# Projections of a hybrid diffusion layer: 26 weight slabs as seven half products of sums in place of eight

## The reference, cut to what matters

```
proj = h @ p["w_in"]                              # h is 384 x 1024
conv_out = _short_conv(proj[..., :D_CONV], ...)   # nine groups of channels, width 3
... hyena, HGRN2, SSD and gated DeltaNet on the parts of proj and conv_out ...
lifted = jnp.einsum("blnc,ncd->blnd", branches, p["w_branch"])
gates = jax.nn.sigmoid(merge).reshape(bsz, L, N_BRANCH, D_MODEL)
mixed = jnp.einsum("blnd,blnd->bld", gates, lifted)
return mixed @ p["w_out"], s_hg, s_ssd, s_gdn
```

## Time and profile before

| | us |
|---|---|
| median of 3 runs | 1486.23 |
| lowest, highest run | 1482.81, 1486.43 |
| span of the profiled execution | 1486.3 |
| PE busy | 1454.8 |
| DVE busy | 463.0 |
| ACT busy | 394.0 |
| POOL busy | 87.4 |

### The profile page before, as it was taken

The page is one execution under the profiler, slowest core; times in us unless marked ns, Lnnn a source line. Parts: engine busy times, 40 slices in busy tenths (PEclk is TensorE's granted clock), DMA queues, the critical chain, the costliest instruction groups (busy, mean ns, idle before and its releaser), DMA issues.

```text
span 1486.3 us, 19276 instructions
## 1 busy us (share of the span) xinstructions
PE 1454.8 (98%) x7422; PEld 914.7 (62%) x7422; DVE 463.0 (31%) x984; ACT 394.0 (27%) x897; POOL 87.4 (6%) x76
## 2 busy tenths in 40 slices
PE   6999999999999999999999999999999999999996
PEld 2565678776786666777865875444555555555553
DVE  3437232663244235323110373211111211221114
ACT  3222112222343233213320232222222222322223
POOL 0000010000021103222111000000000000000001
PEclk9999999999999999999999999999999999999998
DMA  9540423213112328510133335999999898999981
GB/s 372 160 128 8 137 68 113 86 57 113 57 57 86 125 88 308 216 57 29 57 99 118 121 145 210 369 413 382 377 377 382 358 378 355 379 379 380 379 341 43
DMA packets 103944, 308.82 MB, mean 208 GB/s; under 512 B 9168, under 2 KB 69328, under 8 KB 75344
## 3 DMA queue, kind: packets, MB, share of 16 engines
q1 hardware_dynamic: 97552, 304.89, 53.7%
q10 hardware_dynamic: 6336, 3.15, 0.7%
HBM read 304.87 MB, written 3.15 MB: 207 GB/s over the span
## 4 chain that ended last, share of the span: by engine, by line
PE 96%; DMA 2%; DVE 1%; ACT 0%; POOL 0%; issue 0%; SPq 0%; POOLq 0%; DVEq 0%
PE banks L554 43%; PE banks L2480 15%; PE banks L2517 8%; PE banks L2389 7%; PE banks L2381 6%; PE banks L913 4%; PE banks L561 2%; PE banks L1057 1%; PE banks L767 1%; DMA ring<-in_ada_w 1%; PE banks L594 1%; PE banks L662 1%; DMA ring<-in_w_in 1%; PE banks L1105 1%; PE banks L2400 1%; PE banks L657 1%
## 5 line engine op out<-in xcount | busy, mean ns | idle before, releaser
L554 PE MATMUL banks<-hT,ring 128*128 128x384 f32 x1200 | 393.7, 486 | 0.0
L554 PEld LDWEIGHTS banks<-hT,ring 128*128 128x128 f32 x1200 | 226.3, 190 | 153.5 <-issue 2.4
L2480 PE MATMUL banks<-w,xg 128*64 128x512 f32 (+1 forms) x1312 | 234.8, 596 | 0.0
L2480 PEld LDWEIGHTS banks<-w,xg 128*64 128x64 f32 (+1 forms) x1312 | 73.7, 127 | 154.9 <-issue 135.8
L2517 PE MATMUL banks<-w,hidT 128*64 128x512 f32 (+1 forms) x656 | 120.7, 597 | 0.3 <-ACT hidT L2557 0.3
L2389 PE MATMUL banks<-y,selT 128*128 128x512 f32 x384 | 104.4, 407 | 0.0
L2389 PEld LDWEIGHTS banks<-y,selT 128*128 128x128 f32 x384 | 67.3, 188 | 37.7 <-issue 26.2
L554 PE MATMUL banks<-yT,ring 128*128 128x384 f32 x256 | 87.4, 486 | 0.0
L2656 DVE TENSOR_TENSOR y<-banks,y 128x512 fp32r<-128x512 f32 x66 | 45.6, 691 | 133.3 <-ACT y L2573 133.3
L554 PE MATMUL banks<-ring,hT 128*128 128x256 f32 x384 | 86.2, 387 | 0.0
L554 PEld LDWEIGHTS banks<-ring,hT 128*128 128x128 f32 x384 | 74.4, 195 | 10.6
(11 more groups left out here) (404 smaller groups left out, 1478.1 us busy)
## 6 DMA issues: line engine op xcount, KB each, us to landing
w<-in_exp_w SPq DMA_DIRECT2D x198, 1024.0 KB, 8.6
ring<-in_w_in SPq DMA_DIRECT2D x46, 1024.0 KB, 5.4
ring<-in_ada_w SPq DMA_DIRECT2D x24, 1024.0 KB, 7.5
ring<-in_w_branch SPq DMA_DIRECT2D x8, 1024.0 KB, 6.5
ring<-in_w_out SPq DMA_DIRECT2D x4, 1024.0 KB, 6.4
arena<-in_sh_w SPq DMA_DIRECT2D x3, 1024.0 KB, 7.4
arena<-in_t_last_layer SPq DMA_DIRECT2D x1, 1024.0 KB, 8.2
x<-in_x_sample SPq DMA_DIRECT2D x2, 512.0 KB, 11.6
```

The lines of the kernel that those rows point to most:

```text
L554: last = mm(out, lhsT=lhsT, rhs=rhs, start=i == 0, stop=i == len(pairs) - 1)
L2480: ins = mm(ps[lo:hi, :], lhsT=xg[:, k, a_ * P + lo:a_ * P + hi], rhs=w13[:, a_, u, :, k, :], start=k == 0, stop=k == KD - 1)
```

## The change

Both the slab (8 k blocks x 2 channel blocks) and the tokens (8 k blocks x 384 tokens) are cut in two along both sides: weights into a11, a12, a21, a22 (first index channel block, second the half of k), tokens into b11, b12, b21, b22 (half of k, half of the tokens, 192 each). Eight products of halves become seven of sums, in Strassen's way. It is applied to 26 slabs: the two of each of `hy_x1`, `hy_x2`, `ssd_x`, `ssd_bc`, `gdn_k`, `gdn_q`, `gdn_v`, and the four of each of merge 1, 2 and 3. The rest (`hy_v`, merge 0, the `hg` groups, `ssd_z`, `gdn_g`) stays.

A pair is opened and closed on PE. It holds three banks from the first product to the last; each half product is 4 products of 192 columns:

```
+            def open_pair(*name):
+                i = pair_at[name]
+                slab(pe, name)
+                w = blocks(name)
+                pair_banks[name] = y, z, v = banks.hold(pe), banks.hold(pe), banks.hold(pe)
+                half_product(psum[:, v, 0:HALF], w[0][1], hT[:, 4:8, 0:HALF])
+                s_partial.on(half_product(psum[:, y, 0:HALF], w[0][0], hT[:, 0:4, 0:HALF]))
+                pe.wait_ge(s_tokens.sem, 4)
+                pe.wait_ge(s_combos.sem, 4 * i + 1)
+                s_partial.on(half_product(psum[:, z, 0:HALF], w[1][0], token_mix[:, 2]))
+                pe.wait_ge(s_combos.sem, 4 * i + 2)
+                pe.wait_ge(s_kept.sem, 4 * i + 1)
+                s_partial.on(half_product(psum[:, y, 0:HALF], combos[:, 1], token_mix[:, 1], False))
+            def close_pair(*name):
+                i = pair_at[name]
+                w = blocks(name)
+                y, z, v = pair_banks[name]
+                pe.wait_ge(s_kept.sem, 4 * i + 2)
+                half_product(psum[:, z, 0:HALF], w[1][1], token_mix[:, 3], False)
+                pe.wait_ge(s_combos.sem, 4 * i + 3)
+                pe.wait_ge(s_kept.sem, 4 * i + 3)
+                s_partial.on(half_product(psum[:, y, 0:HALF], combos[:, 0], token_mix[:, 0], False))
+                pe.wait_ge(s_combos.sem, 4 * i + 4)
+                pe.wait_ge(s_corner.sem, i + 1)
+                last = half_product(psum[:, v, 0:HALF], w[0][1], hT[:, 4:8, HALF:T])
+                banks.release_all(last, (v, y, z), name, "dve")
+                slab_done(name)
```

```
+            def keep(*name):
+                i = pair_at[name]
+                if i:
+                    banks.emptied(act, PAIRS[i - 1])
+                for n, (bank, to) in enumerate(((0, 0), (1, 1), (0, 2)), 1):
+                    act.wait_ge(s_partial.sem, 4 * i + n)
+                    s_kept.on(on(kept[:, to, :], psum[:, pair_banks[name][bank], 0:HALF], ACT.Copy))
+            def add_up(out, *name):
...
+                dve.wait_ge(s_kept.sem, 4 * i + 1)
+                s_corner.on(tt(out[:, 0, 0:HALF], kept[:, 0, :], v, ALU.add))
+                dve.wait_ge(s_kept.sem, 4 * i + 4)
+                lane.do(tt(out[:, 1, 0:HALF], kept[:, 2, :], z, ALU.add))
+                lane.do(tt(out[:, 1, HALF:T], kept[:, 3, :], kept[:, 1, :], ALU.add))
+                banks.at(dve, name)
+                banks.free(tt(out[:, 0, HALF:T], kept[:, 3, :], v, ALU.add), name)
+            def combine(*name):
...
+                pool.wait_ge(s_slab[at % SLABS].sem, 16 * (at // SLABS + 1))
+                s_combos.on(g.tensor_tensor(a21, a11, a21, ALU.subtract))
...
+                s_combos.on(g.tensor_tensor(combos[:, 1], a22, a21, ALU.subtract))
...
+                s_combos.on(g.tensor_tensor(combos[:, 0], combos[:, 1], a11, ALU.add))
```

In `DELTA_FILL` the merge products become opened and closed pairs, and those of merge 3 begin earlier:

```
-            (1, 0): (("solve", 1, FWD), ("merge", 0)),
-            (1, 1): (("ada_columns", 2), ("lift", 0), ("state", FWD)),
-            (1, 2): (("merge", 1),),
+            (1, 0): (("solve", 1, FWD), ("open", 2, 0)),
+            (1, 1): (("ada_columns", 2), ("close", 2, 0), ("state", FWD)),
+            (1, 2): (("lift", 0), ("lift", 1)),
...
-            (2, 6): (("merge", 7), ("lift", 7)),
+            (2, 5): (("solve", 1, BWD), ("lift", 7)),
+            (2, 6): (("combine", 3, 0), ("open", 3, 0)),
             "end": (("gate", 1), ("solve", 0, FWD), ("solve", 0, BWD), ("out", 1), ("gate", 2), ("out", 2),
-                    ("gate", 0), ("last_state",), ("out", 0), ("turn", 1), ("merge_3", 0), ("turn", 2),
-                    ("merge_3", 1), ("turn", 0))}
+                    ("gate", 0), ("last_state",), ("out", 0), ("turn", 1), ("close", 3, 0), ("turn", 2),
+                    ("turn", 0))}
```

More of the change, by code:

```diff
@@ L159, in release, with release_all @@
         self.close(ins)
+    def release_all(self, ins, taken, key, by):
+        assert self.opened == self.closed
+        while self.turn % 8 in taken:
+            self.turn += 1
+        self.held.difference_update(taken)
+        self.book(taken[0], key, by)
+        for p in taken[1:]:
+            self.last[p] = self.last[taken[0]]
+        self.close(ins)
     def at(self, eng, key):
@@ L396, in trunk @@
+        PAIRED = ("hy_x1", "hy_x2", "ssd_x", "ssd_bc", "gdn_k", "gdn_q", "gdn_v")
+        PAIRS = [(name, h) for name in PAIRED[0:2] for h in range(2)] + [("merge", 1, 0)] + \
+                [(name, h) for name in PAIRED[2:4] for h in range(2)] + [("merge", 1, h) for h in (1, 2, 3)] + \
+                [(name, h) for name in PAIRED[4:] for h in range(2)] + [("merge", n, h) for n in (2, 3) for h in range(4)]
+        pair_at = {name: i for i, name in enumerate(PAIRS)}
         SECOND = {FWD: 2, BWD: 1}
@@ L523, in slab, with blocks, convolved @@
             return ring[:, i % SLABS, :].rearrange("p (k n) -> p k n", k=kd)
+        def blocks(name):
+            w = ring[:, slab_at[name] % SLABS, :].rearrange("p (k n) -> p k n", k=KD)
+            return [[w[:, j * 4:j * 4 + 4, i * P:(i + 1) * P] for j in range(2)] for i in range(2)]
+        def convolved(eng, name):
+            if name in PAIRED:
+                eng.wait_ge(s_convolved.sem, (PAIRED.index(name) + 1) * CW)
+            else:
+                banks.emptied(eng, (name, CW - 1))
         def slab_done(*names):
@@ L581, in project_N, with half_product, pair @@
                 slab_done((name, 0), (name, 1))
+            def half_product(out, w, tokens, start=True):
+                for k in range(KD // 2):
+                    last = mm(out, lhsT=w[:, k, :], rhs=tokens[:, k, :], start=start and k == 0, stop=k == KD // 2 - 1,
+                              skip_group_check=not start)
+                return last
+            def open_pair(*name):
[25 more added lines that the diff above has]
+                slab_done(name)
+            def pair(*name):
+                open_pair(*name)
+                close_pair(*name)
             ada_bank = {}
@@ L719, in _ @@
             for name in ("hy_x1", "hy_x2"):
-                project_T(name, "dve")
+                for h in range(2):
+                    pair(name, h)
             for i, name in enumerate(("hy_v", "hy_x1")):
-                banks.emptied(pe, (name, CW - 1))
+                convolved(pe, name)
                 for t in range(NT):
@@ L891, in _ @@
                     prepare(t + 1)
-                lift(1, 2 * t + 2, 2 * t + 4)
+                pair("merge", 1, t + 1)
+                lift(1, 2 * t + 2, 2 * t + 4, merged=True)
             flip_output(2, sy_out)
             for name in ("gdn_k", "gdn_q"):
-                project_T(name, "dve")
+                for h in range(2):
+                    pair(name, h)
             pe.wait_ge(s_silu.sem, 3)
@@ L1040, in _ @@
             lift(3, 0, 2, merged=True)
-            lift(3, 2, 8)
+            for h in (1, 2, 3):
+                pair("merge", 3, h)
+                lift(3, 2 * h, 2 * h + 2, merged=True)
             pe.wait_ge(s_madd.sem, 3 * KD)
@@ L2033, in _ @@
             fill("end")
-            lift(3, 0, 8)
+            lift(3, 0, 2)
+            for h in (1, 2, 3):
+                add_up(gate, "merge", 3, h)
+                lift(3, 2 * h, 2 * h + 2)
             banks.emptied(dve, ("grow", 2, 1, 1))
+            dve.wait_ge(s_x.sem, 2 * 16 * NT)
             for t in range(NT):
```

259 lines of the change are left out of this document (198 added, 61 removed).

## The result

The changed kernel takes 1506.6 us (median of four runs, 1503.81 to 1509.93) against 1484.99 for the kernel before: a ratio of 1.0148, 95% interval 1.0126 to 1.0171. It is slower by 1.5%. The profiled execution has a span of 1503.8 us, and the run that it comes from took 1505.64, so some 1.8 us lie outside the span. (The median before was 1486.23 of three runs; a fourth makes it 1484.99.)

A forecast was written before the change was run, and what follows sets the result against it. PE, busy 1454.8 of 1486.3 us, bounds the kernel. 1486.3 - 31.5 saved by half products + 32.8 of added PE waits + 3.3 of clock = 1490.9, so 1491; range 1472 to 1506.

The forecast's parts named there:

- half products save: In 26 slabs, 56 records of 192 columns at 162.7 ns replace 32 records: 1.21 us less each, 31.5 in all.
- I put one such fall there: 3.3: At the start of `gdn_k`, the longest added pause brings one stretch of half clock, 3.3 us.
- the clock falls at every pause: Rival: seven long pauses instead of one bring the lower clock, 20 us more, 1511 or 1505; chance 0.10.
- HGRN2's end: Last half of merge (1, 0) waits for its corner, which stands on DVE behind the head norm: 2.3 us.
- SSD's banks: In SSD a pair's three banks include that of `cb`, which DVE frees late: waits of 3.1 and 4.3 us.
- its last pair: SSD's last pair: kept copy behind ACT's square 1.6 us, corner behind a copy, root and `norm_output` 1.05 more.
- the store: At `gdn_k`, 0 ACT first waits for the SSD state's store, delaying PE's kept copy: 5.15 us.
- POOL's copy: At `gdn_k`, 1 a POOL copy of 2.74 us comes ahead of the slab's sums: PE waits 2.85 us.
- the level mask: First level mask: DVE's last key products move behind one more centre and convolution, delaying PE's flips 1.95 us.
- the late slab: Merge (3, 0): its slab's ring slot is free only after lift 7, so PE waits 2.9 us.
- the last corner: Merge (3, 0): its corner stands behind DVE's head norm, a wait of 1.1 us.
- the added work beside PE: Sums and copies on POOL, ACT and DVE are hidden within a dense run of pairs; DVE's busy time up 35 us.

The follow-up runs named there:

- waits_out: Changed kernel with store wait and POOL copy later, banks awaited singly, three corners and lift 7 earlier; 1465.95 us against 1485.45 for the kernel before, ratio 0.9868.
- after_again: The changed kernel itself, nothing altered, executed once more to see its falls of the clock; 1504.3 us.
- after: The changed kernel in its first profiled execution, compared with the kernel before; span 1503.8 us, median of four runs 1506.6 us, ratio 1.0148.

## Why the prediction was wrong, step by step

The sign, slower, was right; 1490.9 was too low by 12.9 us against the span (1503.8), and the median of the runs, 1506.6, lies just outside the range, up to 1506. The terms, measured between the two profiles:

| term of the sum | forecast | measured |
|---|---|---|
| half products save | -31.5 | -28.0 |
| added waits of PE | +32.8 | +31.4 |
| clock | +3.3 | +14.1 |

**The clock failed.** The step was "I put one such fall there: 3.3", with one of 6.7 us in rows 9 as its model. The trace shows seven new falls, behind the pauses at 336, 436, 463, 508, 531, 564 and 729. The longest, 5.12 us, cost 3.0, the others 1.5 to 1.7, together 12.4; the other 1.7 are the routing's, in this pair of profiles. The rival "the clock falls at every pause", with a chance of 0.10, had the number of falls right, seven, but five of the places: none came at `gdn_k`, 1 and SSD's last pair, and two came that it did not list. Its price of 3.3 each was twice what most cost. That the result lies in its 1505 to 1511 is thus in part luck. What I held against it, that PE is fully busy on either side, excludes nothing: the pauses put into dense work of the kernel before show it. The Trainium skill's sentence in "TensorE: Matmul & The Clock Gate" (section "Why this matters for your kernels"), which the prediction named and left to a rival, was the better guide: all 18 pauses of 3.5 us or more in the projections and mixers paid. The runs add that of those of 2 to 3 us about half paid, and not always the same ones. The prediction's own sign, that a span over 1500 with idle time as listed would point to the clock, is what came.

**The waits held, place by place.** Forecast and measured in us: HGRN2's end 2.3 and 2.10; SSD's banks 3.1 and 3.08, 4.3 and 4.40; its last pair 2.65 and 2.41; the store 5.15 and 5.12; POOL's copy 2.85 and 3.01; gdn_v 3.0 and 1.98; the level mask 1.95 and 2.10; the late slab 2.9 and 2.23; the last corner 1.1 and 0.89. Two errors cancel. At `ssd_x` 2.0 were forecast and nothing worth naming came (ACT's first copy ended at 344.70 and PE asked for it at 344.90): ACT loaded the sigmoid's table and took both sigmoids beside the issue of its transfers, where I had added the two. And at gdn_q, 0 I forecast nothing and 3.53 came. It is the step "the added work beside PE": DVE's part was costed as if POOL's did not touch it, 35 us of added busy time where 76.4 were measured. The taps, which had one source in a bank, had both in SBUF after the change. The Trainium skill's "SBUF — State Buffer", section "Who interferes with whom", has the rule: a VectorE instruction with two inputs in SBUF contends with a GpSimd instruction that reads SBUF, and the ports that the two share are an exclusive lock. The traces agree (0.61 us alone, 1.70 beside sums, 3.18 beside the copy; 606 ns once a source lies in a bank).

**The saving was 28.0, not 31.5,** near the 28.6 that the working gave with 2 ns more on each record. In the dense hyena pairs the record takes 162.5 ns, but a pair 9.19 us and not 9.11; these hand-overs and the ends of stretches are the rest. The span against the median: 1.8 us lie outside a span, where I had said nothing does; it is the same in both kernels.

**What was right in the argument** is that the order on the other engines and not the half product decides. waits_out shows it: the same products with 23 us less waiting are 1.3% faster than before.

## To carry to other kernels

Price a pause of the matrix engine at its length and what the clock takes after it, here 1.7 us for more than half of the pauses above 2 us and up to 3 for one of 5; short pauses, even 14 of 0.85 us, cost no more than themselves and 0.27 each. Before a change that ties one engine's product to another engine's copy, list for each place what lies ahead of that copy on its engine: a store's wait, a large fill or a norm that was harmless behind eight free banks costs its full length now, and each could be moved. And when an operand moves from a bank to SBUF, ask what the general engine does meanwhile.

## What the runs showed of the hardware

- Over all profiles with half products and the three with added pauses, the lower clock followed 18 of 18 pauses of PE of 3.5 to 5.1 us in the projections and mixers, 33 of 57 of 1.9 to 3.3 us, 1 of 9 of 1.6 to 1.9 us, and none of 15 of 0.85. Left out of the count are the pause of 1.72 us ahead of the output projection, which no fall followed in any of the 14 profiles, and the pauses of the first 14 us of the kernel: up to 4.6 us long, with little work of PE before them, and the granted clock stays at 1.00 there in all 14. So the length of a pause alone does not decide.
- A fall costs 1.4 to 1.7 us behind pauses up to 4.8 us and 2.3 to 3.0 behind those of 5.0 to 5.1. In the routing it comes in steps near 1.7 us (0, 1.7, 3.4 and 5.1 in different executions of nearly the same code).
- What decides at 2 to 3 us stays open. The place has a part: the pause of 2.7 to 3.1 us at gdn_k, 1 had no fall in any of the six profiles that have it, the one of 3.1 at SSD's first pair had one in all six. But the pause of 2.41 at 487 had one in after_again and none in after, from the same program.
- A DVE instruction with both sources in SBUF waits for a POOL instruction that is under way: 0.61 us alone, 1.70 beside a sum of 1.27, 3.18 beside a copy of 2.74. With one source in a bank the same tap takes 0.61 beside the same copy.
